# Un-normed rows, routing chunk by chunk, another plan of weight buffers, and seven unread matmuls in a two-layer MoE trunk

## The reference

```python
h = h + mixer(rmsnorm(h, attn_norm[layer]), ...)            # ends in from_heads(o) @ w_out
t = rmsnorm(h, ffn_norm[layer])
g_logits = t @ w_group + b_group                             # 4 groups, the best one is taken
e_sel    = (t @ w_router + b_router)[:, best group]          # 8 experts, the best two
gates    = p_group * softmax(top-2 logits)
y        = sum_e  w_down_e . (silu(t @ w_gate_e) * (t @ w_up_e) * gate_e)    # 32 experts, 256 wide
h = h + y
```

## Time and profile before

| | |
|---|---|
| timed runs | 1170.04, 1170.88, 1172.79 us; median 1170.88 |
| profiled execution | 1172.16 us, its span 1170.3 us |
| busy shares | TensorE 87%, its weight loads 47%, VectorE 34%, ScalarE 21%, GpSimd 14% |
| chain that ended last | TensorE 70%, DMA 17%, VectorE 5% |
| moved by DMA | 269.66 MB, mean 230 GB/s |

### The profile page before, as it was taken

How to read it: one execution, slowest core, us unless ns; L and a number is a source line. 1 busy time by engine, 2 the same in 40 slices (tenths; PEclk the granted TensorE clock), 3 DMA queues, 4 the chain that set the end, 5 groups by cost and what they waited for, 6 DMA issues and landing times.

```text
span 1170.3 us, 12919 instructions
## 1 busy us (share of the span) xinstructions
PE 1019.9 (87%) x5132; PEld 549.3 (47%) x5132; DVE 395.4 (34%) x993; ACT 248.9 (21%) x667; POOL 163.5 (14%) x176
## 2 busy tenths in 40 slices
PE   5999999999967999988838998999993999998890
PEld 3344644464444555444414656445452555544440
DVE  3122801272252423212134226457035333221225
ACT  3121701261120010000012226446021010000002
POOL 2000000001002342322110000000002232322210
PEclk9999999999977999999978999999996999998995
DMA  9410202220376999999973212041138799999975
GB/s 331 153 44 30 74 1 72 108 109 24 144 291 255 408 407 411 410 411 411 413 299 113 76 72 73 10 172 63 28 144 354 301 410 410 411 411 410 412 316 226
DMA packets 78973, 269.66 MB, mean 230 GB/s; under 512 B 13568, under 2 KB 17776, under 8 KB 69946
## 3 DMA queue, kind: packets, MB, share of 16 engines
q1 hardware_dynamic: 65904, 243.97, 53.3%
q0 software_dynamic: 13008, 24.85, 5.9%
HBM read 262.44 MB, written 23.10 MB: 244 GB/s over the span
## 4 chain that ended last, share of the span: by engine, by line
PE 70%; DMA 17%; DVE 5%; SPq 3%; ACT 3%; issue 1%; DVEq 0%; ACTq 0%
DMA W<-in_moe_w_up 13%; PE bank L847 13%; PE bank L710 13%; PE bank L796 9%; PE bank L723 9%; PE bank L860 6%; PE bank L736 5%; PE bank L747 3%; PE bank L836 2%; PE bank L763 2%; SPq L406 2%; PE bank L968 2%; PE bank L854 1%; SPq L401 1%; DMA K<-expert_rows 1%
## 5 line engine op out<-in xcount | busy, mean ns | idle before, releaser
L847 PE MATMUL bank<-W,K 128*64 128x256 f32 x896 | 219.7, 401 | 35.0 <-DMA W<-in_moe_w_up 33.3
L848 PE MATMUL bank<-W,K 128*64 128x256 f32 x896 | 219.7, 401 | 0.0
L847 PEld LDWEIGHTS bank<-W,K 128*64 128x64 f32 x896 | 124.5, 144 | 107.6 <-DMA W<-in_moe_w_up 37.7
L710 PE MATMUL bank<-hnT,W 128*128 128x512 f32 x336 | 146.8, 599 | 0.8 <-ACT hnT L1035 0.8
L848 PEld LDWEIGHTS bank<-W,K 128*64 128x64 f32 x896 | 124.5, 144 | 0.0
L1424 DVE SCALAR_TENSOR_TENSOR PT<-bank,V,PT 64x256 f32<-64x256 f32 x64 | 31.4, 491 | 271.1 <-ACT PT L1100 271.0
L796 PE MATMUL bank<-W,oT 128*128 128x512 f32 x256 | 111.2, 594 | 1.4 <-ACT oT L1079 1.4
L860 PE MATMUL bank<-D,PT 128*64 128x512 f32 x224 | 108.0, 604 | 0.7 <-ACT PT L1103 0.7
L862 PE MATMUL bank<-D,PT 128*64 128x512 f32 x224 | 108.0, 604 | 0.0
L710 PEld LDWEIGHTS bank<-hnT,W 128*128 128x128 f32 x336 | 64.1, 192 | 81.6 <-issue 80.6
L723 PE MATMUL bank<-W,hnT 128*128 128x512 f32 (+2 forms) x320 | 100.8, 475 | 1.6 <-DVE K L1524 1.6
(11 more groups left out here) (214 smaller groups left out, 1187.3 us busy)
## 6 DMA issues: line engine op xcount, KB each, us to landing
W<-in_moe_w_gate SPq DMA_DIRECT2D x56, 1024.0 KB
W<-in_moe_w_up SPq DMA_DIRECT2D x56, 1024.0 KB
D<-in_moe_w_down SPq DMA_DIRECT2D x56, 1024.0 KB
W<-in_e_w_in SPq DMA_DIRECT2D x5, 2048.0 KB
hnT<-in_moe_w_down SPq DMA_DIRECT2D x8, 1024.0 KB
W<-in_e_w_out SPq DMA_DIRECT2D x2, 2048.0 KB
hn_rows<-Q POOLq DMA_DIRECT2D x8, 512.0 KB, 3.5
oT<-in_moe_w_gate SPq DMA_DIRECT2D x4, 1024.0 KB
```

The source lines that it names most:

```text
L710: last = nc.tensor.matmul(b[:, :], w[:, k, 128 * fb:128 * fb + 128], hnT[:, k, :], start=(k == 0), stop=(k == KD - 1))
L847: nc.tensor.matmul(bank[2 + e2][0:64, 0:256], xt, w[:, at:at + 256], start=first, stop=end)
L848: last = nc.tensor.matmul(bank[2 + e2][64:128, 0:256], xt, w[:, 2048 + at:2304 + at], start=first, stop=end)
```

## The change

- **Rows without norm.** `h` itself is transposed and multiplied with the router, whose weights are scaled once by the norm's gain (`wr`); each token's inverse root is applied to the logits (`choose`). `h` itself is written to DRAM and gathered; the gain goes into the copy of the transposed rows (`rows_in`), the roots into silu's scale (`rtab`) and the slot weights.
- **Routing by chunk**, inside `mixer_out` and `mixer_add`: as soon as a chunk has its logits, VectorE chooses (`choose`, with running maxima by scan instead of maximum, compare and minimum) and places (`place`) it, and TensorE does its `ranks` and `slots` between the products.
- **Seven matmuls** of the identity with the constant table into bank 1, which nothing reads (`stay_busy`): 2 of 512 columns, 1 of 256, 4 of 512.
- **Buffers.** The output weights are loaded into Q and K once the last scores are made. Six buffers serve the experts up to 23, four the last eight. Loads of experts 0 to 3 go out earlier; 4 during the mixer's second half, 5 after it, their down weights after the first gather. The latent projection's weights go into oT during the last experts.
- `records`, needed only for further passes, moves into expert 1.

```diff
-            def experts(lay):
-                base = NE * lay
-                for s in range(4):
-                    slot_free(T_MOE[lay] + s)
-                    load_gate_up(lay, s)
-                    load_down(lay, s)
-                sp.wait_ge(s_og, 8 * (lay + 1))
-                load_gate_up(lay, BESIDE[0])
+            def before_routing(lay, w_out):
+                sp.wait_ge(s_qk, 64 * (lay + 1))
+                load_cols("Q", flatQ.rearrange("p (k n) -> p k n", k=KD), w_out, 0, 512)
+                load_cols("K", flatK.rearrange("p (k n) -> p k n", k=KD), w_out, 512, 512)
+                sp.wait_ge(s_pv, 8 * (lay + 1))
+                load_down(lay, 3)
+                sp.wait_ge(s_og, 8 * lay + 4)
+                load_gate_up(lay, 4)
+                rows = h_dram[lay].rearrange("(s h) d -> s (h d)", h=2)
+                for c in range(C):
+                    sp.wait_ge(s_oga, 8 * lay + 5 + c)
+                    sp.dma_start(rows[128 * c:128 * c + 128, :], h[:, c, :]).then_inc(s_hst, 16)
+                sp.wait_ge(s_og, 8 * lay + 8)
+                load_gate_up(lay, 5)
+                sp.wait_ge(s_g[0], 16 * (8 * lay + 1))
                 sp.wait_ge(s_lg, C * (lay + 1))
-                load_down(lay, BESIDE[0])
-                sp.wait_ge(s_hnst, 64 * (lay + 1))
-                load_gate_up(lay, BESIDE[1])
-                load_down(lay, BESIDE[1])
+                load_down(lay, 4)
+                load_down(lay, 5)
...
+                def stay_busy(times, width):
+                    for _ in range(times):
+                        nc.tensor.matmul(bank[1][:, 0:width], ident, cst[:, 0:width], start=True, stop=True)
+
+                pe.wait_ge(s_oev, 8 * (lay + 1))
+                for half, buf in enumerate("QK"):
+                    pe.wait_ge(*landed(buf, ("out", 2 * lay + half)))
+                    for c in range(C):
+                        product(half, c, 0, 1)
+                        if half:
+                            if c:
+                                second_half(c - 1)
+                            else:
+                                first_half(3)
+                        elif c:
+                            first_half(c - 1)
+                        product(half, c, 1, 3)
+                        if half and c == 3:
+                            slots(0)
+                        if half and c >= 2:
+                            ranks(c - 2)
+                        product(half, c, 3, 4)
+                        if half and c:
+                            logits(c - 1, 0)
+                            logits(c - 1, 1)
+                        product(half, c, 4, 6)
+                        if half and c == 3:
+                            logits(3, 0)
+                        product(half, c, 6, 8)
+                second_half(3)
+                slots(1)
+                ranks(2)
+                logits(3, 1)
+                stay_busy(2, 512)
+                slots(2)
+                ranks(3)
+                stay_busy(1, 256)
+                slots(3)
...
+                last.then_inc(s_ws, 1)
+                stay_busy(4, 512)
...
             def experts(lay):
                 base = NE * lay
+                act.wait_ge(s_wt, lay + 1)
                 for e in range(NE):
                     act.wait_ge(s_gu, base + e + 1)
-                    silu(e % 2, s_sil)
+                    silu(e % 2, rtab[0:64, e:e + 1], s_sil)
...
+                for c in range(C):
+                    add(1, c)
+                    rows_t_out(c)
+                    root_inverse(2 * lay + 1, c)
+                    if c:
+                        place(c - 1)
+                    choose(c)
+                place(C - 1)
...
             def experts(lay):
                 base = NE * lay
                 dve.wait_ge(s_xt, base + 1)
-                nc.vector.tensor_copy(XT[0], bank[0][:, :]).then_inc(s_xte, 1)
+                rows_in(0, s_xte)
+                spread_ranks(lay)
```

More of the change, by code:

```diff
@@ L92, in trunk @@
     X = mybir.AxisListType.X
-    hn_dram = [nc.dram_tensor(f"hn_rows{l}", (2 * S, DM // 2), f32, kind="Internal").ap() for l in range(2)]
+    h_dram = [nc.dram_tensor(f"rows{l}", (2 * S, DM // 2), f32, kind="Internal").ap() for l in range(2)]
     tab_dram = [nc.dram_tensor(f"expert_table{l}", (S * NE, 4), i32, kind="Internal").ap() for l in range(2)]
@@ L712, in project_features, with project_rows @@
                     last.then_inc(s_pj, 1)
[L714 to L717 removed]
+            def project_rows(w, ready, c0, width, per_group, chunks=range(C)):
+                pe.wait_ge(*ready)
                 for c in chunks:
@@ L825, in routing @@
                                             start=(n == 0), stop=(n == 2 * C - 1))
-                last.then_inc(s_slots, 1)
-            def weights_to_slots(lay):
-                pe.wait_ge(s_facts, 4 * lay + 4)
-                for n in range(2 * C):
-                    last = nc.tensor.matmul(bank[7][:, 160:192], rank_hot32[:, n, :], wfacts[:, n, :],
-                                            start=(n == 0), stop=(n == 2 * C - 1))
-                last.then_inc(s_slots, 1)
+                last.then_inc(s_ws, 1)
@@ new lines, in place @@
+                def place(c):
+                    dve.wait_ge(s_rank, 4 * lay + c + 1)
+                    for k in range(2):
+                        ins = nc.vector.tensor_tensor_reduce(out=pick[k], in0=bank[7][:, 32 * c:32 * c + 32],
+                                                             in1=oh[k][:, c, :], scale=1.0, scalar=0.0,
+                                                             op0=ALU.mult, op1=ALU.add, accum_out=rpos[k][:, c:c + 1])
+                    then(ins)
+                    for k in range(2):
+                        ins = nc.vector.tensor_scalar(rank_hot[:, C * k + c, :], cst[:, C_RANK:C_RANK + 128],
+                                                      rpos[k][:, c:c + 1], None, ALU.is_equal)
+                    ins.then_inc(s_facts, 1)
@@ new lines, in mixer_add @@
+                nc.vector.memset(gstep[:, 0:1], 0.0)
+                nc.vector.memset(estep[0][:, 0:1], 0.0)
+                nc.vector.memset(estep[1][:, 0:1], 0.0)
+                then(nc.vector.tensor_copy(tri_ones, cst[:, C_TRI:C_ONE + 128]))
+                for c in range(C):
+                    add(0, c)
+                dve.wait_ge(s_small, (112, 272)[lay])
+                nc.vector.tensor_tensor(wr, wr, router_gain.unsqueeze(2).to_broadcast([128, KD, 36]), ALU.mult)\
+                  .then_inc(s_wr, 1)
```

594 lines of the change are left out of this document (325 added, 269 removed).

## The result

The changed kernel takes 1150.68 us (median of 4 runs, 1149.53 to 1156.07) against 1170.97 (4 runs, 1170.04 to 1172.79): the ratio is 0.9835, with an interval from 0.9817 to 0.9852. 1151.5 was predicted. Timed again among the experiments it took 1151.73 against 1170.32, ratio 0.9848 [0.983, 0.9865]. Its profiled execution took 1149.53 (span 1147.7), that of before 1172.16 (span 1170.3).

A forecast was written before the change was run, and what follows sets the result against it. Expert stage taken as bound by transfers, 232 us from its first load's trigger. Earlier triggers -20.4, given back +1.0: -19.4 from 1172.16 gives 1152.8 profiled; timed median 1.28 lower, 1151.5 us; range 1145.5 to 1160.

The forecast's parts named there:

- trigger + 232 us: Expert stage: its last down product comes 232 us after expert 6's load leaves, when gate_up(0) has ended.
- T' = T + 5.9: Mixer: its last product, added by VectorE, ends 5.9 us later after the change (T') than before (T).
- From T' to POOL, 9.3: Routing: from the changed mixer's last product to POOL's first gather takes 9.3 us.
- choose(3): Routing of the last chunk on VectorE: 12 dependent steps and the sum, 2.9 us, ending at +6.7.
- slower: Rival, mixer's second half: VectorE becomes the bound, about 1200 us; chance 0.03.
- The gather, 2.4: First gather of expert rows: running alone it takes 2.4 us, landing 11.7 us after the mixer's last product.
- the gather's 6.6 us is its own: Rival, first gather: it stays 6.6 us without neighbours, costing 2.0 us a layer, 1155.5 us; chance 0.09.
- The four matmuls, ended at +13.9: Last four unread matmuls before expert 0: they end 13.9 us after the mixer's last product, between +12.2 and +15.6.
- the clock holds: Rival, after the mixer: TensorE stays at 2.4 GHz, four matmuls end at +12.2, 1.7 us less a layer, 1148; chance 0.17.
- The trigger, T' + 19.2: End of gate_up(0), when expert 6's load leaves: 19.2 us after the changed mixer's last product.
- Given back, 0.5 a layer: Expert 0: a silu and small copy before hidden(0) delay the load after gate_up(1) by 0.5 us a layer.
- bytes come late: Rival, weight loads: Q lands with K, 4.2 us a layer, or down 4 and 5 spill over; 1160 us; chance 0.08.

The follow-up runs named there:

- half-down kernel: Changed kernel with only the first of down's two parts done in experts 8 to 23, all bytes still loaded; 1153.77 us, ratio 0.9851.
- halves: Changed kernel with the loads of experts 6 and 7 each cut in two, the first part leaving earlier; 1150.67 us, ratio 0.9816.
- first three only: Changed kernel without the last four of the seven unread matmuls; 1155.47 us, ratio 0.988.
- ten: Changed kernel with ten unread matmuls of 512 columns in place of the last four; 1162.57 us, ratio 0.9928.
- weights beside the gather: Changed kernel with expert 5's gate/up load held back until the slots are filled, just before the first gather; 1163.54 us, ratio 0.9932.
- none: Changed kernel without any of the seven unread matmuls; 1156.72 us, ratio 0.9883.
- last four only: Changed kernel without the first three of the seven unread matmuls; 1155.80 us, ratio 0.9882.
- the fill: Kernel before the change with unread matmuls alone added, three behind the logits and seven behind the slot products; 1168.79 us, ratio 0.997.

## Why the prediction was right

**The stage is trigger + 232 us.** Held: 232.7 and 232.1 to the last down product's copy (584.80, 1120.06), forecast 232 to 233. By the last scatter it is 232.4 to 234.4 in every kernel above whose expert 1 keeps its clock, but for one layer. The half-down kernel is what shows that bytes set it; but its layer 1 took 236.2. Why its bytes came later there is open: TensorE's low clock doesn't explain it, since in layer 0 the clock was lower (0.76 from 460 to 485) and the stage took 233.8. The rule needs a second term: where expert 1 runs at half clock, 1.4 to 2.0 us more (3.8 in the layer with halves).

**T' = T + 5.9** was too small: 66.0 against 58.8 us from the mixer's start, + 7.2. The added pieces among the products take 7.2 where 5.8 were summed up from groups timed alone. That cost 1.3 us a layer. Some 1.0 of it is in the seven groups of four transposes: the second stands for 0.58 us between two products (277.51 + 6.87 to 284.96 in the chain), where 0.44 was summed.

**From T' to POOL, 9.3**: measured 8.8. choose(3) took 3.1 us (338.27 to 341.39) where 2.9 was forecast, but began at + 3.4, not + 3.8. VectorE was late in no chunk: T' follows TensorE's own products, and the rival "slower" had nothing to stand on.

**The gather, 2.4** of bounds 2.4 to 6.7: measured 3.10 and 2.95. The rival "the gather's 6.6 us is its own" is refuted both ways: without neighbours it takes 3.3 and 2.8 in the kernel before, and with them 7.1 and 6.7 in the changed one. The Trainium skill, DMA: Bandwidth & Descriptors, section Queues, rings and completion order, has each engine go round its queues packet by packet. That alone would not make a small gather wait for the megabytes that were issued 0.7 us ahead of it, and here it did, by 4 us. How the engines shared out the packets is not shown, so why the neighbour costs 4 us stays open. Alone, the gather took 2.8 to 3.4 us in all kernels whose chain shows it, so 2.4, the scatter's time, was too little.

**The four matmuls, ended at +13.9**: this is where the sum was most off. The clock did fall, as forecast, but at T' + 3, so that the first two unread matmuls ran at 1.2 GHz, and it came back before the last four. These took 3.68 us and ended at + 11.7, as in the rival "the clock holds" (+ 12.2). The prediction counted the first three as costing nothing and bringing nothing; they bring 1.2 and 1.5 us (18.5 and 18.6 against 17.3 and 17.2).

**The trigger, T' + 19.2**: measured 17.3 and 17.2. With T' 1.3 late that leaves 0.6 and 0.7 us a layer more gain than forecast (11.0 and 10.8 against 10.4 and 10.0). The forecast had two errors that nearly cancel: T' 1.3 us too early, and the four matmuls' end 2.2 us too late. That the median came out within 0.8 us of it is in part luck; the way the time is gained (trigger, shorter gather, gate_up(0) at full clock) is as forecast.

**Given back, 0.5 a layer**: 0.3 and 0.7. SyncE's second load follows the first by 7.9 us instead of 7.3.

**The output weights in Q and K** cost nothing that shows: in the changed kernel's chain the first product, at 268.87, waits for ScalarE's copy into oT (268.22 + 0.61), not for Q. But Q's load left at 260.75, and in the chains of two variants ("first three only" and "ten") it is the step just before the mixer, 8.17 and 8.11 us long, with the mixer at the same 8.1 to 8.3 us behind the load. So it takes some 8.1 us to be landed, not 7.1, the margin is nil, and the rival "bytes come late" was near. The 7.1 was the end of the earlier load's traffic; in "first three only" the traffic too has moved Q's 2.1 MB some 7.2 us behind the issue (268.2). What fills the last microsecond, the notice of the landing or packets of K's load, which stands right behind, isn't shown.

By the experiments, the 20.3 us are: some 14 from everything but the seven matmuls, of which the gather's empty neighbourhood is 6 when put into the kernel before alone and 12 to 13 when taken out of the changed one; and 5 to 6 from the seven matmuls (ten of them bring 3 in the kernel before). The parts don't add up: with a late gather TensorE idles ahead of gate_up(0) in the changed kernel and comes to it at half clock, while in the kernel before it does so anyway. Un-normed rows, routing by chunk and the new buffers were not tried one by one; of them only the stretches of the traces tell, with 5.0 and 4.5 us for the earlier gather.

## What to carry to other kernels

Where a stage is full of transfers, look for the event that starts it, and price a change by what it does to that event alone; its length behind the event can then be checked against the trace of before. A small gather on the path should have no large load issued in front of it: issue that load earlier or after, not with it. If TensorE waits a few microseconds ahead of a stretch where its speed decides, unread matmuls that end just before the awaited data pay for themselves, but only if they do not outlast the wait; put some early, to bring the clock back, and some late, to keep it.

## What the runs showed of the hardware

- Where TensorE idled 4.05 and 4.27 us for the gathered rows, the clock fell just before that time or within it, and gate_up(0) began at 1.2 GHz; where the four wide matmuls ran at 2.4 GHz until just before the rows came and it idled 0.26, gate_up(0) ran at 2.4 GHz.
- A gather of an expert's rows took 2.8 to 3.4 us alone and 6.1 to 7.1 us when megabytes of weights, issued before it on another queue, were still on their way.
- The same instructions can keep or lose the clock: two executions of the changed kernel differ in layer 1 (0.50 for some microseconds in one, 1.00 throughout in the other) behind T', and behind a wait of 1.39 us in expert 0 the clock fell in both layers of two kernels ("ten" and "weights beside the gather") and in layer 0 of the one with halves, but not in its layer 1, nor in the changed kernel, "none", "last four only", "first three only" and "half of down left out". In the kernel before this wait is 0.81 us and the clock held; with the fill it fell. Which it will be could not be told from the rows ahead.
- With less work, TensorE had a granted clock of 0.81 instead of 0.97 in a stretch of 50 us, so that its busy share hardly fell (43.5 to 42.7 us). A busy share without the clock beside it says little about how near an engine is to its bound.
